# Maxima of the third attention group from rounded 64-row operands, with its queries copied by DMA

## The reference, cut to what matters

```python
s = jnp.einsum('brhcqe,brhcke->brhcqk', qb, kb) * (E ** -0.5)
s = jnp.where(valid, s, -jnp.inf)
m = jnp.max(s, axis=-1)
p = jnp.exp(s - m[..., None])
l = jnp.sum(p, axis=-1)
o = jnp.einsum('brhcqk,brhcke->brhcqe', p, vb)
...
wts = jnp.exp(ms - jnp.max(ms, axis=0))
den = jnp.sum(wts * jnp.stack(dens), axis=0)
num = jnp.sum(wts[..., None] * jnp.stack(outs), axis=0)
o_b = (num / den[..., None])
```

## Time and profile before

| | |
|---|---|
| median of 3 runs | 1507.05 us (1506.86 to 1507.41) |
| the profiled execution | 1506.9 us, span 1505.0 us |
| PE busy | 1487.3 us, 99% of the span |
| DVE busy | 856.2 us, 57% |
| ACT busy | 704.7 us, 47% |
| granted TensorE clock | 1.000 |

### The profile page before, as it was taken

One profiled execution on the slowest core, in us unless ns is written; L12 is line 12 of the kernel. 1 busy time (PEld: TensorE's weight loads), 2 busy tenths in 40 slices (PEclk: granted clock), 3 DMA queues, 4 the chain that ended last, 5 costly groups with the idle time before them and its releaser, 6 DMA issues. The chain is left out here.

```text
span 1505.0 us, 21090 instructions
## 1 busy us (share of the span) xinstructions
PE 1487.3 (99%) x7920; PEld 1270.9 (84%) x7920; DVE 856.2 (57%) x1389; ACT 704.7 (47%) x877; POOL 33.4 (2%) x39
## 2 busy tenths in 40 slices
PE   7999999999999999999999999999999999999998
PEld 6888888888888888888888888888888888888987
DVE  6746565563746374667952586258635865644523
ACT  5747566565647473745522534244434435411212
POOL 0100000000000000001400000000000000000000
PEclk9999999999999999999999999999999999999999
DMA  5121211121111211122313212321232134333702
GB/s 217 43 70 57 69 37 61 56 70 56 57 55 56 70 56 56 56 70 76 89 48 98 58 41 74 88 68 36 79 85 71 32 104 140 113 120 101 260 32 84
DMA packets 35520, 116.84 MB, mean 78 GB/s; under 512 B 6200, under 2 KB 6520, under 8 KB 35448
## 3 DMA queue, kind: packets, MB, share of 16 engines
q1 hardware_dynamic: 35456, 115.94, 24.0%
HBM read 83.21 MB, written 20.02 MB: 69 GB/s over the span
## 5 line engine op out<-in xcount | busy, mean ns | idle before, releaser
L690 PE MATMUL z_ps<-h_hi,w_hi 128*128 128x512 f32 x1376 | 545.1, 396 | 0.6 <-ACT zz L1181 0.6
L692 PE MATMUL z_ps<-h_hi,w_lo 128*128 128x512 f32 x1376 | 536.6, 390 | 0.0
L691 PE MATMUL z_ps<-h_lo,w_hi 128*128 128x512 f32 x1376 | 536.1, 390 | 0.0
L692 PEld LDWEIGHTS z_ps<-h_hi,w_lo 128*128 128x128 f32 x1376 | 258.2, 188 | 55.0
L690 PEld LDWEIGHTS z_ps<-h_hi,w_hi 128*128 128x128 f32 x1376 | 258.7, 188 | 51.6 <-issue 1.6
L691 PEld LDWEIGHTS z_ps<-h_lo,w_hi 128*128 128x128 f32 x1376 | 258.7, 188 | 49.8
L1331 DVE TENSOR_TENSOR w_lo<-w_stage,w_hi 128x1024 fp32r<-128x1024 f32 x89 | 109.4, 1229 | 224.4 <-ACT w_hi L1015 224.1
L1024 ACT ACT_TABLE_LOAD x61 | 78.3, 1283 | 74.6 <-PE z_ps L692 73.8
L1129 ACT ACTIVATE pt<-pb 128x512 f32<-128x512 f32 (+1 forms) x80 | 43.5, 543 | 119.5 <-PE pb L836 119.1
L1015 ACT ACTIVATE w_hi<-w_stage 128x1024 fp32r<-128x1024 f32 x89 | 93.8, 1054 | 0.3
L853 PE MATMUL pc<-pt,vb 128*128 128x128 f32 x560 | 77.6, 279 | 1.2 <-ACT pt L1129 1.2
(11 more groups left out here) (268 smaller groups left out, 2231.0 us busy)
## 6 DMA issues: line engine op xcount, KB each, us to landing
w_stage<-w_in SPq DMA_DIRECT2D x88, 512.0 KB, 3.4
z_swap<-zz SPq DMA_DIRECT2D x96, 128.0 KB, 2.3
gate_d<-gate SPq DMA_DIRECT2D x16, 512.0 KB, 4.5
x_in<-x SPq DMA_DIRECT2D x8, 512.0 KB, 7.6
o_a_d<-o_a SPq DMA_DIRECT2D x8, 512.0 KB, 4.8
w_stage<-w_a SPq DMA_DIRECT2D x8, 512.0 KB, 3.7
cos_t<-gate_d SPq DMA_DIRECT2D x8, 512.0 KB, 4.5
sin_t<-gate_d SPq DMA_DIRECT2D x8, 512.0 KB, 3.6
```

Source lines behind the costliest of these rows:

```text
L690: nc.tensor.matmul(z_ps[hf][:], w_hi[s][:, k, :], h_hi[:, k, t], start=k == 0, stop=False)
L691: nc.tensor.matmul(z_ps[hf][:], w_hi[s][:, k, :], h_lo[:, k, t], start=False, stop=False)
L692: last = nc.tensor.matmul(z_ps[hf][:], w_lo[s][:, k, :], h_hi[:, k, t], start=False, stop=k == KT - 1)
```

## The change

For group 2, DVE adds the rotated queries in place in `zz[0]`, one instruction on 128 rows (slot 12). SP then issues the four exchange DMAs of the keys, behind them two DMAs of 64 rows that copy `zz[0]` into the halves of `q_sh[2][h]` (semaphore `q2_copied`; the wait for the scores of the pair before moves from DVE to SP), and behind these the weight load that stood ahead of the exchange. ACT waits for `q2_copied` and no longer for `rope_sum` before it writes v into `zz[0]`. At slot 14 ACT rounds both halves into the free halves of the other head's tile (two copies of 64 rows, `q2_rounded`), and DVE adds the keys three times: two 64-row sums into `k_sh`, and a 128-row sum rounded to f32r in place in `zz[1]` (`k_hi2`). At slot 16 PE multiplies operands of 64 rows, head 0 in the upper and head 1 in the lower half of the rows, alternately, in f32r. POOL's clearing of rows goes, and so do two of its fills; SP waits once for POOL's fills before the first pair's rows.

```diff
-            sides[name][g][h] = place(f"{name}{g}{h}", [P, SEQ], f32r if g < 2 else f32)
+            sides[name][g][h] = place(f"{name}{g}{h}", [P, SEQ], f32 if (name, g) == ("k_sh", 2) else f32r)
...
+        top[0] = zz1_at
+        k_hi2 = place("k_hi2", [P, SEQ], f32r)
...
-                    if cur:
+                    if cur and c != 6:
                         split = value(sp, n + 1)
...
+                        if c == 6:
...
+                            if prev:
+                                scored = value(sp, i * N_UNITS)
+                                sp.wait_ge(const_in, 32)
+                                sp.wait_ge(st_made, scored)
+                            for h in range(2):
+                                rows = slice(EDIM * h, EDIM * (h + 1))
+                                sp.dma_start(q_sh[2][h][rows, :].bitcast(f32), zz[0][rows, :]).then_inc(q2_copied, 16)
+                            split = value(sp, n + 1)
+                            sp.wait_ge(const_in, 32)
+                            sp.wait_ge(w_lo_done, split)
+                            load_stage(n + 2, c % 2)
...
+            def maxima_of_both(i, m):
+
+                pe.wait_ge(q2_rounded, i * 2 + 2)
+                pe.wait_ge(rope_sum, i * 6 + 6)
+                if max_bank(i, 2, m) is pc and not first(i):
+                    pe.wait_ge(ob_taken, i * N_SUMS)
+                else:
+                    pe.wait_ge(mx_taken, i * N_MAX + max_count(14 + 2 * m if first(i) else 16))
+                for blk, at, _ in max_queries(2, m):
+                    cols = slice(P * blk, P * blk + P)
+                    for h in range(2):
+                        rows = slice(EDIM * h, EDIM * (h + 1))
+                        last = nc.tensor.matmul(max_bank(i, 2, m)[:, h, at:at + P], q_sh[2][1 - h][rows, cols], k_hi2[rows, cols], start=True, stop=True)
...
+                    if cur and slot == 14:
+
+                        act.wait_ge(q2_copied, i * 32 + 32)
+                        for h in range(2):
+                            rows = slice(EDIM * h, EDIM * (h + 1))
+                            nc.scalar.activation(q_sh[2][1 - h][rows, :], q_sh[2][h][rows, :].bitcast(f32), ACT.Copy).then_inc(q2_rounded, 1)
...
                             if g == 0 and hf == 0:
-                                act.wait_ge(rope_sum, i * 6 + 5)
+                                act.wait_ge(q2_copied, i * 32 + 32)
...
+                    if cur and slot == 12:
...
+                        nc.vector.tensor_tensor(zz[0][:], zz[0][:], z_swap[:], ALU.add).then_inc(rope_sum, 1)
+                    if cur and slot == 14:
...
                         for h in range(2):
                             rows = slice(EDIM * h, EDIM * (h + 1))
-                            dst = (q_sh, k_sh)[j % 2][2][h]
-                            last = nc.vector.tensor_tensor(dst[rows, :], zz[j % 2][rows, :], z_swap[rows, :], ALU.add)
-                        last.then_inc(rope_sum, 1)
+                            last = nc.vector.tensor_tensor(k_sh[2][h][rows, :], zz[1][rows, :], z_swap[rows, :], ALU.add)
+                        last.then_inc(k2_summed, 1)
+                        dve.wait_ge(k2_summed, i + 1)
+                        nc.vector.tensor_tensor(k_hi2[:], zz[1][:], z_swap[:], ALU.add).then_inc(rope_sum, 1)
```

More of the change, by code:

```diff
@@ L201, in build @@
             place_side(name, g, h)
-        zz = [place(f"zz{s}", [P, SEQ]) for s in range(2)]
+        zz = [place("zz0", [P, SEQ])]
+        zz1_at = top[0]
+        zz.append(place("zz1", [P, SEQ]))
         z_swap = place("z_swap", [P, SEQ])
@@ L319, in build @@
         MASKS = 9
[L320 removed]
+        PADS = 17
         N_BR = HEADS + PAIRS
@@ L433, in rows_to_queries @@
             def rows_to_queries(i):
+                if first(i):
+                    sp.wait_ge(padded, PADS)
                 for g in range(GROUPS):
@@ L501, in attention @@
                             sp.dma_start(z_swap[32 * q:32 * q + 32, :], zz[(c - 1) % 2][32 * o:32 * o + 32, :]).then_inc(swapped, 16)
+                        if c == 6:
+                            if first(i):
+                                sp.wait_ge(oa_stored, 16 * HEADS)
+                                for s in range(2):
+                                    sp.wait_ge(gate_stored[s], 16 * HEADS)
+                            if prev:
[9 more added lines that the diff above has]
+                            load_stage(n + 2, c % 2)
                     if first(i) and c == 4:
@@ L610, in pad_group @@
                     as_f32 = lambda ap: ap.bitcast(f32) if g < 2 else ap
-                    pad(as_f32(q_sh[g][h][other, :]), 0.0)
+                    if g < 2:
+                        pad(as_f32(q_sh[g][h][other, :]), 0.0)
                     pad(as_f32(k_sh[g][h][other, :]), 0.0)
@@ L622, in _ @@
             assert pads[0] == PADS
-            for i in range(1, PAIRS):
-                seen, cleared = value(pool, i * N_UNITS), value(pool, i * 2 - 1)
-                pool.wait_ge(const_in, 32)
-                pool.wait_ge(st_made, seen)
-                nc.gpsimd.memset(q_sh[2][0][EDIM:EDIM + 1, :], 0.0).then_inc(row_cleared, 1)
-                pool.wait_ge(row_cleared, cleared)
-                nc.gpsimd.memset(q_sh[2][1][0:1, :], 0.0).then_inc(row_cleared, 1)
         @block.tensor
@@ L792, in maxima @@
                     pe.wait_ge(mx_taken, i * N_MAX)
[L793 to L800 removed]
+                pe.wait_ge(qk_lo_done, i * 4 + 2 * g + 2)
+                pe.wait_ge(q_dupped, i * 4 + 2 * g + h + 1)
                 for blk, at, before in max_queries(g, m):
                     lo = blk - 1 if before else blk
[L803 to L806 removed]
+                    at += 0 if before else P
+                    last = nc.tensor.matmul(max_bank(i, g, m)[:, h, at:at + P * (blk + 1 - lo)], q_two[g][h][:, P * blk:P * blk + P],
+                                            k_two[g][h][:, P * lo:P * blk + P], start=True, stop=True)
                 last.then_inc(mx_made, 1)
+            def maxima_of_both(i, m):
[10 more added lines that the diff above has]
+                        last = nc.tensor.matmul(max_bank(i, 2, m)[:, h, at:at + P], q_sh[2][1 - h][rows, cols], k_hi2[rows, cols], start=True, stop=True)
+                        if blk == 4 * m + 3:
+                            last.then_inc(mx_made, 1)
             def scores_t(i, u):
@@ L835, in scores_t @@
                         nc.tensor.matmul(dst, k_two[g][h][:, ks], q_two[g][h][:, qs], start=False, stop=False)
-                    last = nc.tensor.matmul(dst, k_sh[g][h][:, ks], q_sh[g][h][:, qs], start=False, stop=blk == units[-1][0])
+                    q_side = q_sh[g][h][:, qs] if g < 2 else q_sh[g][h][:, qs].bitcast(f32)
+                    last = nc.tensor.matmul(dst, k_sh[g][h][:, ks], q_side, start=False, stop=blk == units[-1][0])
                 last.then_inc(st_made, 1)
@@ L885, in attention @@
                         for g, m in MAX_SLOTS.get(slot, ()):
-                            for h in range(2):
-                                maxima(i, g, m, h)
+                            if g == 2:
+                                maxima_of_both(i, m)
+                            else:
+                                for h in range(2):
+                                    maxima(i, g, m, h)
                     if cur and slot == 17:
```

29 lines of the change are left out of this document (8 added, 21 removed).

## The result

The changed kernel takes 1514.01 us (median of 4 runs, 1513.42 to 1514.81) against 1507.23 us (1506.86 to 1507.89) of the kernel before beside it: ratio 1.0045, 95% interval 1.0032 to 1.0057. My forecast was 1507.6 us, and the time lies above the end of my range, 1511.8. The profiled execution took 1513.4 us with a span of 1511.5 us, 6.5 us more than the span of before, at a mean clock of 0.996 instead of 1.000.

A forecast was written before the change was run, and what follows sets the result against it. PE was taken to bound the kernel, busy 1487.3 of 1505.0 us. Saving -8.1, slot 14 waits coming back -0.9 and new waits +9.7 gave +0.7 on 1506.9: 1507.6 us, range 1502.0 to 1511.8.

The forecast's parts named there:

- my D + 9.4: Weight load behind the copies: lands near D + 9.4, in time for slot 16; D is the start of DVE's query sum.
- What should come back at slot 14: Slot 14's maxima in pairs 1 to 3: their 0.3 us waits for DVE go, 0.9 us for three pairs.
- My 9.7 us: Start of slot 14: PE waits behind ACT's v copy 3.06, 2.22, 2.21 and 2.21 us, 9.7 us in all.
- my 1.23 + 0.09 + 4.14 = 5.46: Ahead of slot 14, from D, DVE's query sum start: sum 1.23, to SP's first issue 0.09, four exchanges 4.14 us.
- my D + 7.96: Ahead of slot 14: both query copies landed, 2.5 us at 205 GB/s behind the exchange; D starts DVE's query sum.
- My 1.55 us for a pair's maxima: Slot 16: 1.35 us for 16 records plus 0.2 for tiling changes, against 3.57; saves 2.02 a pair, 8.1 in all.
- a case of mine at 1.1 us: Slot 16, heads overlap fully: 0.91 + 0.2 us a pair, saving 9.8, 1505.9 us; part of the forecast's case.
- The slower one (1511.4): Rival, slot 16: 64-row matmuls keep full pitch and drain at both edges, 2.5 us a pair; 1511.4 us; chance 0.20.
- The faster one: Rival, slot 14: copies land early, overlapping the exchanges, second before D + 7; waits 4.6, 1502.5 us; chance 0.26.
- its bound of D + 7.4: Slot 14: PE's earliest start if copies pass without queueing, landing 2.3 us after issue; waits 4.6 us in all.
- the forecast's D + 8.70: Slot 14: when PE can begin, counted from D, the start of DVE's query sum, after copies and ACT's v copy.
- The one in which nothing is saved: Rival, slot 16: 64-row f32r operands run as two records at the old pitch; 8.8 us lost, 1515.7 us; chance 0.03.

## Why the prediction was wrong

**The frame held.** The trade was the one I described: a saving at slot 16 against a wait at slot 14 behind the query copies. Everything I costed at nothing cost nothing: the rounding copies, the weight load (11.2 us of waits with it ahead, 11.3 behind), the third key sum, POOL, the transpose of `m_all`. The first weight load behind the copies came later than my D + 9.4 (ACT's split of it waited for it until 757.18, D + 10.4), still in time for slot 16. PE's 0.6 us were not all its waits in that window, since there were 0.2 us more behind DVE's row maxima, which changes nothing. What should come back at slot 14 did, though less of it, 0.65 us instead of 0.9: 0.31 and 0.29 in pairs 1 and 2, but the four matmuls took only 0.51 in pair 3 before, not the 0.77 of the earlier trace rows that I used for all three.

**The step that failed is one that is not there.** I wrote that "a wait in which PE has nothing to do lengthens it by its whole length". It lengthened it by more: behind waits of 2.5 to 3.4 us the clock fell to half for a part of slot 14, 1.7 us each time, three times in four pairs, 5.2 us in all (7.1 us instead of 5.4 for the same matmuls). The run with work inside the wait gives 5.1 us back and shows the idle time as the cause. The attention of the kernel before has no PE wait over 1.2 us (the longest, behind `pt`, in the last pair), so its rows there hold no price for it; but I didn't ask what the clock does when PE stops, and had no rival for it. The end of the same trace held the sign. PE's last matmul is over at 1499.7, and the clock falls with nothing on PE:

```profile
1499.80:1504.70 4.90, 0.00 (x0) 1.00 0.55 214
1504.80:1505.00 0.20, 0.00 (x0) 0.50 0.00 0
```

With this term my sum would have been +5.9, 1512.8 us. The Trainium skill, "TensorE: Matmul & The Clock Gate", section "What's actually happening", states that the clock is set by how busy TensorE has been recently and has two levels; the traces here agree, and a rival could have been drawn from it.

**The wait was under-sized.** My 9.7 us measured 11.8. The steps up to DVE's go held (D + 5.50 against my 1.23 + 0.09 + 4.14 = 5.46), and so did the two after the landing (0.74). The term that was off is the copies' own: 512 KB at the 205 GB/s of the exchange, 2.5 us. They took 2.96 in pair 0 and ACT's copy began at D + 8.40, 8.35 and 8.81 in the others, against my D + 7.96. I had taken the rate of a stretch of the exchange; the copies reached 177 GB/s. Whether the weight load issued right behind them took a part of the path stays open. That the six transfers share one full path was right: with the order turned round or two queues at once they end within 0.5 us of each other. But what made the copies late in the change was mostly their later issue, 2.4 us, and their own 3.5 us; the exchange ahead of them and not behind added about 0.2.

**The saving was under-sized.** My 1.55 us for a pair's maxima, "the middle" of 0.91 and 1.79 with 0.2 for the change of tiling, measured 1.04 and 0.15 at the edges, 1.19 together: 9.5 us saved instead of 8.1. By its parts it is 0.88 for the matmuls and 0.3 for the two changes of tiling, so the first term was 0.47 too high and the second 0.1 too low. For the second I had looked at changes between f32 and f32r, which are not changes of rows. The heads overlap fully, which was a case of mine at 1.1 us, edges included; the middle between two ends of which only one mechanism decides was no estimate. That its 0.91 came so near to 0.88 is luck: it stood for 16 matmuls at 0.057 us one after another, and what passes is eight couples at 0.11. The Trainium skill, "TensorEngine Tiling (Array Packing)", "Key Properties", says that tiles work in parallel and that a change of tiling mode drains the engine. The traces bear out the first, with 2.75 and 1.98 us for the same unrounded matmuls in the two orders; whether the 0.3 us a pair at the changes are a drain they don't show. The rule of "TensorE: Matmul & The Clock Gate", "LDWEIGHTS (loading the stationary operand)", in the Trainium skill, that a weight load takes its columns at 1.2 GHz, so 0.107 us for 128, agrees with the 0.11 us from one couple of matmuls to the next; what I drew from it, 16 loads one after the other, does not, since two in different rows run at once.

**The rivals.** The slower one (1511.4) gave the right sign for a wrong reason: a pair's records took 1.04 us and not over 2.1, since the full pitch held for couples and not for single matmuls, and the changes of tiling cost 0.3 us and not 0.7. The faster one fell with the landing at D + 8.46, and it had less room than I gave it: its bound of D + 7.4 used 2.3 us from issue to landing, the median of an exchange of 128 KB, where a copy of 256 KB took 3.1 us at the least and 3.5 at the median with the exchange behind it. With 3.5 in place of 2.3 my early bound would have been about D + 8.6 (an estimate), next to the forecast's D + 8.70. The one in which nothing is saved fell with the 16 records.

The errors are +5.2 for the clock, +2.1 for the wait, +0.25 for what comes back and -1.4 for the saving, together +6.1; the forecast missed by 6.4, of which 0.3 is the base: I started from 1506.9 us, and the kernel before took 1507.2 beside the change.

## What to carry to other kernels

When an edit puts a long wait in front of a TensorE that otherwise never stops, price the wait and then the clock behind it: here 2.5 to 3.4 us of idle time cost 1.7 us more in three of four cases, and useless matmuls in the wait were worth 5.1 us. Ask which buffer ties the wait to TensorE: half a tile of 2 KB a partition took the copies off the path and turned +6.8 us into -10.4. And try the cheapest half of an idea by itself: the two heads on different rows of the array, in alternation, gave 6.0 us with no rounding, no copies and no new semaphore.

## What I had not expected of the hardware

- Two matmuls on rows 0 to 63 and 64 to 127 enter together, rounded or not, even four places apart in the program: 1.09 us a pair with four of one head in a run, 1.04 in alternation.
- Rounded matmuls of 128 rows and 128 columns came eight in 0.93 to 1.04 us with the change to 64 rows included, no faster than eight records of the unrounded ones (0.89).
- Going from 128 rows to 64 and back cost about 0.3 us a pair, half of it outside the maxima.
- The clock at its lower level in 10 of 13 cases behind idle times of 2.25 to 3.40 us, and in none of twelve behind idle times of 0.2 to 1.7 us; which pair is spared changed when the same waits came 1 to 3 us later.
- Six transfers within SBUF of 1.05 MB took 6.7 to 7.2 us from the first issue whether one queue issued them in either order or two queues at once; with two queues an issue on SP took 1.0 us on average instead of 0.6, and with the copies ahead on the same queue 0.75.
